# Thirty-two experts in an order found on the chip, the two largest run twice on one set of weights

## The chip, the cores and the metric

The kernel runs on one core of one Trainium2 chip. The metric is device time in microseconds (us) of one execution; lower is better. TensorE (PE in the profile) multiplies, PEld is its weight load, VectorE is DVE, ScalarE is ACT, GpSimd is POOL, and SyncE (SP) issues most DMAs.

## The reference, cut to what matters

The reference runs two transformer layers and a third block that ends in a mixture of experts. Only the mixture is touched. 512 tokens choose 4 of 32 experts each, so there are 2048 rows of work, and an expert with more than 128 tokens needs more than one block of 128 rows:

```python
logits = (xt @ router_w + router_b).astype(jnp.float32)
top_logits, top_idx = lax.top_k(logits, TOP_K)
gates = jax.nn.softmax(top_logits, axis=-1)
...
hmid = xt[tok] @ w_gu[e] + b_gu[e]             # 1024 -> 2048
glu = jnp.minimum(hmid[:, 0::2], SWIGLU_LIMIT)
lin = jnp.clip(hmid[:, 1::2], -SWIGLU_LIMIT, SWIGLU_LIMIT)
act = glu * jax.nn.sigmoid(SWIGLU_ALPHA * glu) * (lin + 1.0)
return act @ w_down[e] + b_down[e]             # 1024 -> 1024
```

All is float32. With the inputs of the reference the router gives expert 10 152 tokens and expert 12 130; eleven more experts have 65 to 124, and nineteen have 64 or fewer.

## The kernel before

The mixture is `experts`. `out_norm_and_route` finds the gates, each token's place in its expert (`T.place`) and the counts (`T.counts`, as integers `T.count`). `first_blocks` runs the first 128 tokens of experts 0 to 31 in their own order. `extra_blocks` runs what is left over, and `combine_and_finish` fetches four result rows for each token, adds them with the gates and normalises.

An expert's weights are six units of 2 MB (`expert_unit`): 0 to 3 are the two halves of the up projection, 4 and 5 the down projection. They go through a ring of eight slots (`ring_view`, `Home`); the first slot is named `unit_whole`. SP loads unit n of the next expert when the unit that held the slot, eight loads earlier, is used (`unit_used`, L4183).

An expert is one step, and each engine branches in it on the count (`is_half`, a register loaded from `T.count`, L4198). With 64 tokens or fewer the step is a **half** step: `up_half` and `down_half` multiply plain float32 in two column groups of 64 at once. Otherwise it is a **parted** step: unit 0 is multiplied in plain float32 (L3900), units 1 to 5 as three products of parts that ACT rounds (L88) and DVE subtracts (L91), quarter by quarter (L3870, L3871, L3875). Expert 0 alone has an unparted full path, `up` and `down`, in plain float32.

Rows of the next expert are fetched by an indirect DMA of POOL (L3575) and turned by PE (`turn_rows`, L3590), one half behind the up projection and one behind the turning of the activations (L3711 in a half step, L3883 in a parted one). `find_tokens` (L3559) makes the index three experts ahead.

The loop stands in `in_rounds`: experts 0 to 3 written out, a `Fori` over six rounds of four, experts 28 to 31 written out. While expert 0 is waited for, DVE works out which extra blocks there are (`Extras.find`, `find_jumps`). An extra block loads all six units of its expert again: for the first one SP issues them behind expert 31's, for a second one as the first's are used. The extra blocks' loop always makes 15 passes and skips those that are not needed.

Of the kernel before, what the change touches and what calls it, by code (L numbers as in the profile page):

```python
# [5 lines left out]
ALU = mybir.AluOpType  # L6
# [8 lines left out]
P = 128  # L15
# [1006 lines left out]
def mlp(k, i, gain, clear_rows=False):  # L1022
# [15 lines left out]
    with ExitStack() as ctx:  # L1038
# [19 lines left out]
        with k.block() as block:  # L1058
# [35 lines left out]
            def _(act):  # L1094
                if clear_rows:
                    act.wait_ge(k.pool_made.sem, k.pool_made.at(1))
                for n, (u, is_up, j) in enumerate(order):
                    k.round_unit(act, u + 1)
                    if clear_rows:
                        rows = k.rows[3 * n:min(3 * n + 3, BLOCKS)].rearrange("b p d -> p b d")  # L1100
                        act.dma_start(rows, zero[:, :, :].broadcast_to([P, rows.shape[1], D])).then_inc(k.rows_cleared, 16)
# [2362 lines left out]
BLOCKS = EXPERTS + MOST_EXTRA  # L3464
# [3 lines left out]
SLOTS = 8  # L3468

# [32 lines left out]
class Experts:  # L3502


    def __init__(self, k, name, tables, one_by_one):
# [6 lines left out]
        self.loaded = [signal(f"loaded{r}") for r in range(SLOTS)]  # L3512
        self.sel_ready = signal("sel_ready")
        self.index_full = signal("index_full")
        self.index_ready = signal("index_ready")
        self.fetched = [signal(f"rows_fetched{r}") for r in range(2)]
# [16 lines left out]
    def make_sel(self, dve, j, par):  # L3533
# [4 lines left out]
        for t in range(TT):  # L3538
            ins = dve.tensor_scalar(T.sel[:, par, t, :], T.iota[:, :], T.place[:, t, bass.ds(j, 1)], None, ALU.is_equal)
# [95 lines left out]
    def save_act(self, act, j):  # L3635
        k, T = self.k, self.tables
        act.wait_ge(self.act_turned, 2 * j + 2)
        act.activation(T.actT[:, :, :].rearrange("p (b f) s -> p b (f s)", b=2), k.psum[:, 4:6, :], ACT.Copy)\
           .then_inc(self.actT_ready, 2)
# [33 lines left out]
    def up(self, pe, j, home, xg, par):  # L3673

        k, T = self.k, self.tables
        for pair in range(2):
            for r in range(2):
                w = home.wait(pe, 2 * pair + r)
                for g in range(2):
# [4 lines left out]
                    for c in range(HALF_K):  # L3684
                        pe.matmul(bank, xg[:, HALF_K * r + c, :], w[:, c, g * 512:(g + 1) * 512],
                                  start=(r == 0 and c == 0), stop=False)
# [101 lines left out]
    def down(self, pe, j, home, par):  # L3788
        k, T = self.k, self.tables
        self.wait_for_down(pe, j)  # L3790
        for r in range(2):
            w = home.wait(pe, 4 + r)
            for half in range(2):
                bank = k.psum[:, 6 + half, :]
                cols = slice(half * 512, (half + 1) * 512)
                for c in range(HALF_K):
                    pe.matmul(bank, T.actT[:, HALF_K * r + c, :], w[:, c, cols], start=(r == 0 and c == 0), stop=False)
# [207 lines left out]
def experts(k):  # L4005

    with ExitStack() as ctx:
# [3 lines left out]
        T.place = k.sb("moe_place", [P, TT, BLOCKS], ctx=ctx)  # L4011
        T.iota = k.sb("moe_iota", [P, P], ctx=ctx)
# [5 lines left out]
        T.count = k.sb("moe_count", [P, EXPERTS], I32, ctx=ctx)  # L4018
# [7 lines left out]
        T.index = k.sb("moe_index", [P, EXPERTS], I32, ctx=ctx)  # L4026
# [9 lines left out]
        with ExitStack() as inner:  # L4036
# [21 lines left out]
            first_blocks(k, base, T, extras, later)  # L4058
# [4 lines left out]
class Extras:  # L4063
# [4 lines left out]
    def __init__(self, k, T, ctx):  # L4068
        self.k, self.T = k, T
        self.known = k.ctx.enter_context(k.nc.semaphore("extras_known"))  # L4070
        self.flag = k.sb("extra_flag", [P, ROUNDS - 1, EXPERTS], ctx=ctx)
# [18 lines left out]

    def find(self, dve):
# [5 lines left out]
        step(ins)  # L4097
        dve.memset(self.zero[:, :], 0.0)
# [18 lines left out]
    def fill(self, dve, t):  # L4117
# [5 lines left out]
        k.dve.step(dve, self.look_up(dve, self.cand[:, 0], T.place[:, t, EXPERTS:BLOCKS]))  # L4123

    def find_jumps(self, dve):
# [5 lines left out]
        step(dve.tensor_tensor(self.jump[:, 1, :], order[:, 0, :], T.ids[:, :], ALU.subtract))  # L4131
        step(dve.tensor_scalar(self.jump[:, 1, :], self.jump[:, 1, :], float(EXPERTS - 1), float(P), ALU.add, ALU.mult))
        step(dve.tensor_tensor(self.jump[:, 2:, :], order[:, 1:, :], order[:, :-1, :], ALU.subtract))
# [19 lines left out]
def first_blocks(k, E, T, extras, later):  # L4153
# [3 lines left out]
    PER_ROUND = 4  # L4157
    rounds = EXPERTS // PER_ROUND
    k.unit_rounded.passed(len(k.units))
    k.unit_split.passed(len(k.units))  # L4160
    with k.block() as block:
        def in_rounds(eng, step):

            for b in range(PER_ROUND):
                step(0, b, b, True, False)
            with eng.Fori(1, rounds - 1) as i:
                for b in range(PER_ROUND):
                    step(i, b, PER_ROUND * i + b, False, False)
            for b in range(PER_ROUND):
                step(rounds - 1, b, PER_ROUND * (rounds - 1) + b, False, True)  # L4170

        @block.sync
        def _(sp):
            def step(i, b, j, first, last):
                if last and b == PER_ROUND - 1:
                    return
# [565 lines left out]
```

## Time and profile before

| | us |
|---|---|
| median of 3 runs (lowest, highest) | 3099.53 (3092.92, 3102.09) |
| the profiled execution | 3098.87 |
| its span, first to last instruction | 3097.1 |
| experts 1 to 31, from store to store of the results | 1023.9 |
| the two extra blocks | 96.0 |

The page of the profile gives busy time of each engine (PE 89% of the span, DVE 52%, ACT 34%), the span in 40 slices, the chain of work that ended last, and the costliest groups of instructions. In a row of a timeline the first number is the start, the second the duration, and square brackets hold the engine's idle time before the row and who ended it. The issue of a result store on ACT is taken as the end of a step.

### The profile page before, as it was taken

How to read it: one execution, taken by the hardware profiler on the slowest of the kernel's cores; microseconds unless marked ns; L12 is line 12 of the kernel's file. 1: busy time of each engine (PE TensorE's matmuls, PEld its weight loads, DVE VectorE, ACT ScalarE, POOL GpSimd, SP SyncE). 2: the span in 40 equal slices, each digit the busy share in tenths (PEclk: the TensorE clock that was granted, in tenths of full speed). 3: DMA queues.
4: the chain of work that ended last, by engine and by line, in shares of the span. 5: the costliest groups of instructions: out<-in, count | busy, mean ns of one | idle time of the engine just before them, and what ended most of it. 6: DMA issues, size and time to landing. Idle time of an engine off the chain costs nothing. (4 is left out here: it accounts for less than half of the span.)

```text
span 3097.1 us, 35668 instructions
## 1 busy us (share of the span) xinstructions
PE 2741.5 (89%) x13162; PEld 1970.5 (64%) x13163; DVE 1614.4 (52%) x2447; ACT 1047.0 (34%) x1464; POOL 193.8 (6%) x213
## 2 busy tenths in 40 slices
PE   7877999999999899999966876998989998899962
PEld 6655778888878788888754663553655455455530
DVE  4864545444555544446855536652855454464413
ACT  4444443322224432233333231330634233343301
POOL 0530000000000000000012130000000000000002
PEclk9988999999999999999976787999999999999986
DMA  3110314444233132322210038999999999999974
GB/s 131 58 51 28 109 62 177 171 169 183 101 120 111 66 116 82 109 82 71 103 60 1 1 122 329 404 414 414 413 385 380 361 412 370 414 412 395 415 291 151
DMA packets 192096, 638.46 MB, mean 206 GB/s; under 512 B 12413, under 2 KB 18204, under 8 KB 191522
## 3 DMA queue, kind: packets, MB, share of 16 engines
q1 hardware_dynamic: 173856, 579.61, 48.7%
q10 hardware_dynamic: 11106, 39.11, 3.2%
q0 software_dynamic: 6912, 16.68, 1.4%
q8 instruction: 151, 2.47, 0.3%
q14 instruction: 71, 0.58, 0.1%
HBM read 600.61 MB, written 43.25 MB: 208 GB/s over the span
## 5 line engine op out<-in xcount | busy, mean ns | idle before, releaser
L91 DVE TENSOR_TENSOR unit_low<-unit_whole,unit_high 128x4096 fp32r<-128x4096 f32 (+3 forms) x95 | 287.8, 3035 | 174.8 <-ACT unit_high L88 172.9
L669 PE MATMUL psum<-tokens_high,unit_high 128*128 128x512 f32 (+2 forms) x1016 | 372.5, 367 | 4.4 <-PEq L865 1.6
L669 PE MATMUL psum<-tokens_high,unit_low 128*128 128x512 f32 (+2 forms) x1016 | 368.7, 363 | 0.0
L669 PE MATMUL psum<-tokens_low,unit_high 128*128 128x512 f32 (+2 forms) x1016 | 368.6, 363 | 0.0
L88 ACT ACTIVATE unit_high<-unit_whole 128x4096 fp32r<-128x4096 f32 (+2 forms) x65 | 225.8, 3474 | 374.2 <-PE psum L669 291.3
L91 DVE TENSOR_TENSOR moe_low<-ring_slot,moe_w_high 128x1024 fp32r<-128x1024 f32 x228 | 266.7, 1219 | 19.4 <-ACT moe_w_high L88 18.4
L88 ACT ACTIVATE moe_w_high<-ring_slot 128x1024 fp32r<-128x1024 f32 x228 | 236.5, 1055 | 61.4 <-PE psum L3875 60.4
L3698 PE MATMUL psum<-ring_slot,hT 128*64 128x512 f32 x1136 | 251.9, 594 | 0.0
L669 PEld LDWEIGHTS psum<-tokens_high,unit_high 128*128 128x128 f32 (+1 forms) x1016 | 191.0, 188 | 37.9 <-DVE unit_low L91 4.0
L669 PEld LDWEIGHTS psum<-tokens_low,unit_high 128*128 128x128 f32 (+1 forms) x1016 | 191.1, 188 | 31.6 <-issue 1.6
L669 PEld LDWEIGHTS psum<-tokens_high,unit_low 128*128 128x128 f32 (+1 forms) x1016 | 191.0, 188 | 30.6 <-issue 0.2
L669 PE MATMUL psum<-unit_high,hidden_high 128*128 128x512 f32 x512 | 199.7, 390 | 0.0
L669 PE MATMUL psum<-unit_high,hidden_low 128*128 128x512 f32 x512 | 199.4, 389 | 0.0
L669 PE MATMUL psum<-unit_low,hidden_high 128*128 128x512 f32 x512 | 199.4, 389 | 0.0
L3741 DVE TENSOR_SCALAR moe_glu<-psum 128x256 f32<-128x256 f32 x42 | 17.8, 425 | 324.4 <-PE psum L3704 232.7
L3698 PEld LDWEIGHTS psum<-ring_slot,hT 128*64 128x64 f32 x1136 | 83.5, 137 | 148.9 <-issue 147.7
L3726 PE MATMUL psum<-ring_slot,moe_actT 128*64 128x512 f32 x640 | 155.8, 641 | 9.7 <-ACT moe_actT L3766 9.7
L1147 DVE TENSOR_TENSOR x_residual<-psum,x_residual 128x512 f32<-128x512 f32 x128 | 84.4, 687 | 117.7 <-PE psum L669 117.7
L3870 PE MATMUL psum<-moe_w_high,moe_xg_high 128*128 128x512 f32 x312 | 131.1, 420 | 0.0
L3755 ACT ACTIVATE moe_sig<-moe_glu 128x256 f32<-128x256 f32 x42 | 17.5, 416 | 316.0 <-DVE moe_glu L3741 316.0
L3871 PE MATMUL psum<-moe_low,moe_xg_high 128*128 128x512 f32 x312 | 122.1, 391 | 0.0
L1137 DVE SCALAR_TENSOR_TENSOR hT<-psum,hidden_relu 128x512 f32<-128x512 f32 x64 | 43.8, 689 | 147.3 <-ACT hidden_relu L1109 147.3
(646 smaller groups left out, 4908.9 us busy)
## 6 DMA issues: line engine op xcount, KB each, us to landing
ring_slot<-in_moe_w_gu SPq DMA_DIRECT2D x118, 2048.0 KB, 19.4
ring_slot<-in_moe_w_down SPq DMA_DIRECT2D x60, 2048.0 KB, 20.5
unit_whole<-in_moe_w_gu SPq DMA_DIRECT2D x18, 2048.0 KB, 16.9
unit_whole<-in_w_up SPq DMA_DIRECT2D x16, 2048.0 KB, 7.5
unit_whole<-in_w_down SPq DMA_DIRECT2D x16, 2048.0 KB, 7.7
expert_rows<-zero_row ACTq DMA_DIRECT2D x15, 1536.0 KB, 5.3
unit_whole<-in_moe_w_down SPq DMA_DIRECT2D x8, 2048.0 KB, 19.7
unit_whole<-in_w_in SPq DMA_DIRECT2D x5, 2048.0 KB, 7.7
```

The source lines that it names most:

```text
L88: return act.activation(self.high, self.whole, ACT.Copy)
L91: return dve.tensor_tensor(self.low, self.whole, self.high.bitcast(F32), ALU.subtract)
L669: ins = pe.matmul(bank, a, c, start=(first and m == 0), stop=(last and m == len(parts) - 1))
L1137: dve.scalar_tensor_tensor(out=hidden[j % 2].whole[:, b, :], in0=bank, scalar=0.0, in1=relu[:, h % 2, :], op0=ALU.max, op1=ALU.mult)\
L1147: dve.tensor_tensor(x, bank, x, ALU.add).then_inc(k.bank_free.sem, 1)
L3698: ins = pe.matmul(banks[g], xg[:, c, 0:HALF], w[c // HALF_K][:, c % HALF_K, g * 512:(g + 1) * 512], start=(c == 0), stop=False)
L3726: ins = pe.matmul(banks[g], T.actT[:, c, 0:HALF], w[c // HALF_K][:, c % HALF_K, g * 512:(g + 1) * 512], start=(c == 0), stop=False)
L3741: dve.tensor_scalar(T.glu[:, pair, :], bank[:, :, 0], 7.0, None, ALU.min).then_inc(self.glu_ready, 2)
L3755: act.activation(T.sig[:, pair, :], T.glu[:, pair, :], ACT.Sigmoid, scale=1.702).then_inc(self.gate_ready, 2)
L3870: pe.matmul(banks[g], a.high[:, f, :], w.high[:, cols], start=(first and q == 0), stop=False)
L3871: pe.matmul(banks[g], a.high[:, f, :], w.low[:, cols], start=False, stop=False)
```

## The change

1. DVE sorts the experts by count on the chip (`put_in_order`): compare each with each (32x32), sum, and pick expert and count for each of 34 steps by a table of ranks. Results are the integer tables `T.order`, `T.column`, `T.count`, and a semaphore `ordered`.
2. There are 34 steps. Step 0 is expert 0 as before. Steps 2 and 3 are both the largest expert, steps 29 and 30 both the second largest; step 3 and step 30 run its tokens from the 129th on, with the weights that are still in the ring. From step 4 to 28 large and small experts take turns.
3. Steps 2, 3, 29 and 30 are of kind "whole": a full one is multiplied by `up` and `down` in plain float32 instead of in parts.
4. SP, ACT and DVE load the expert's number into a register in each step (`expert_at`, `column_at`).
5. PE turns both halves of the next rows behind the up projection.
6. Extra blocks are only those beyond the two second blocks; their prefetch in `first_blocks` is gone.

```diff
+AT_SECOND = (3, STEPS - 4)
+RANKS = [EXPERTS - 1, 26, 0, 0, 27] + [r for m in range(12) for r in (2 + m, 14 + m)] + [1, 1, 28, 29, 30]
...
+    for q, b, kind in ((0, 0, "first"), (1, 1, "parted"), (2, 2, "whole"), (3, 2, "whole"), (4, 3, "parted")):
+        step(Step(q, 0, b, kind))
+    with eng.Fori(1, ROUND_LAST) as i:
+        for b in range(PER_ROUND):
+            step(Step(PER_ROUND * i + b + 1, i, b, "parted"))
+    for q, b, kind in ((0, 0, "whole"), (1, 0, "whole"), (2, 1, "parted"), (3, 2, "parted"), (4, 3, "parted")):
+        step(Step(STEPS - 5 + q, ROUND_LAST, b, kind))
...
+        def expert_at(eng, q):
+            return eng.value_load(T.order[0:1, bass.ds(q, 1)], min_val=0, max_val=EXPERTS - 1)
...
+            sp.wait_ge(extras.ordered, 1)
+            load(Home(E, 0, 1), 1, (None, 0))
+            load(Home(E, 0, 2), 2, (0, 1))
+            load(Home(E, 0, 3), 4, (1, 3))
+            load(Home(E, 0, 4), 5, (3, 4))
...
-                    E.turn_rows(pe, j + 1, 0, 1 - par, (PER_ROUND // 2) * i + (b + 1) // 2 + 1)
+                if s.has(1):
+                    E.turn_rows(pe, q + 1, 0, 1 - par, s.fetches())
+                    E.turn_rows(pe, q + 1, 1, 1 - par, saved=q + 3 if s.has(2) else STEPS)
                 with pe.If(half):
-                    E.turn_act_half(pe, j)
+                    E.turn_act_half(pe, q)
+                    E.down_half(pe, q, home, par, counted)
...
+            E.make_sel(dve, 0, 0, 0)
             E.save_tokens(dve, 0)
+            E.make_bias(dve, 0, 0)
+            extras.put_in_order(dve)
+            E.make_sel(dve, 1, 1, column_at(dve, 1))
             E.save_tokens(dve, 1)
...
+                elif s.kind == "first":
+                    rows = 0
+                else:
+                    rows = expert_at(act, q)
```

What this moves, engine by engine. **PE, one step of the loop**, on its half path. Before, behind the up projection's bias (L3704), `hT` in L3590 being the next rows and L3711 the turning of the activations:

```order
L3590 MATMUL psum<-ident,hT 128x128 x4
L4226 COMPARE_AND_BRANCH
L3709 REGISTER_ALU
L3711 MATMUL psum<-ident,moe_act 128x128 x4
...
L3590 MATMUL psum<-ident,hT 128x128 x4
L4235 COMPARE_AND_BRANCH
```

After, in the same place, where L3626 turns the rows and L3752 the activations:

```order
L3626 MATMUL psum<-ident,hT 128x128 x4
L3622 REGISTER_ALU
L3626 MATMUL psum<-ident,hT 128x128 x4
L4326 COMPARE_AND_BRANCH
L3750 REGISTER_ALU
L3752 MATMUL psum<-ident,moe_act 128x128 x4
```

The second four turnings have moved ahead of the branch, and one branch of three is gone. **DVE, the start of the expert stage**, before; `moe_sel` is the one-hot table of an expert's tokens and `moe_index` its list:

```order
L3539 TENSOR_SCALAR moe_sel<-moe_iota,moe_place 128x128 x8
L3566 TENSOR_SCALAR moe_index<-psum 128x1 x2
L3539 TENSOR_SCALAR moe_sel<-moe_iota,moe_place 128x128 x4
L3597 COPY moe_bias_ones<-moe_bias_pick 128x128
L3605 TENSOR_TENSOR hT<-psum,feature_vectors 128x512 x2
```

And after:

```order
L3602 TENSOR_SCALAR moe_index<-psum 128x1
L3633 COPY moe_bias_ones<-moe_bias_pick 128x128
L4149 SCALAR_TENSOR_TENSOR extra_order<-moe_counts,moe_ids 128x32
L4151 MEMSET extra_order 128x1
L4152 TENSOR_TENSOR extra_prod<-extra_order 128x1024
L4154 TENSOR_REDUCE moe_rank<-extra_prod 128x32
L4156 TENSOR_TENSOR extra_prod<-moe_rank,moe_ranks 128x1088
L4158 TENSOR_TENSOR extra_prod<-extra_prod,moe_ids 128x1088
L4159 TENSOR_REDUCE moe_by_step<-extra_prod 128x34
```

The ordering stands between the first expert's index and the second expert's table, and the first expert's rows are saved (`hT`) behind both. **ACT, between two steps of the loop**, before and then after; L3650 and L3689 issue the store of the last results:

```order
L3650 DMA expert_rows<-moe_o 128x1024
L4315 UNCONDITIONAL_BRANCH
L4198 ISA
L4198 TENSOR_LOAD moe_count
L4198 ISA x2
L4311 COMPARE_AND_BRANCH
```

```order
L3689 DMA expert_rows<-moe_o 128x1024
L4415 UNCONDITIONAL_BRANCH
L4262 ISA
L4262 TENSOR_LOAD moe_order
L4262 ISA x2
L4259 REGISTER_ALU
L4259 TENSOR_LOAD moe_count
L4259 ISA x2
L4411 COMPARE_AND_BRANCH
```

A second register load stands ahead of the step's first activation.

## Rows read from the trace of the kernel before

**Rows 1.** Waits of PE, 1925.7 to 2949.6: us in total, times, longest

```profile
PE psum L3711 <- DVE moe_act L3748: 29.6, 18, 2.2
PE psum L3875 <- DVE moe_actT_low L3944: 11.8, 13, 1.0
PE psum L3870 <- ACT moe_actT_high L3979: 11.7, 13, 0.9
PE psum L3900 <- issue: 11.2, 3, 3.8
PE psum L3726 <- ACT moe_actT L3766: 9.0, 17, 0.8
PE psum L3698 <- issue: 5.6, 2, 3.8
```

**Rows 2.** Stretches: bounds, length, busy PE, PEld, DVE, ACT, POOL, then clock, DMA share, GB/s

```profile
1925.70:2949.60 1023.90, 943.68 (x4206) 530.89 (x4202) 539.57 (x863) 373.07 (x459) 31.57 (x29) 0.98 1.00 399
...
2047.90:2088.00 40.10, 38.25 (x166) 27.38 (x166) 32.40 (x39) 25.03 (x27) 1.23 (x1) 1.00 1.03 415
...
2113.90:2141.10 27.20, 23.79 (x114) 9.67 (x110) 5.66 (x17) 2.67 (x6) 0.99 (x1) 0.94 1.02 412
...
2556.80:2602.50 45.70, 41.32 (x168) 28.74 (x170) 32.63 (x39) 24.92 (x27) 1.23 (x1) 0.96 0.96 365
...
2857.10:2882.50 25.40, 23.46 (x114) 8.53 (x111) 4.78 (x13) 2.67 (x6) 0.99 (x1) 1.00 1.03 413
...
2949.60:3045.60 96.00, 64.30 (x340) 33.79 (x340) 11.40 (x30) 5.55 (x13) 0.00 (x0) 0.86 0.52 207
3045.60:3056.10 10.50, 0.00 (x0) 0.00 (x0) 0.00 (x0) 0.20 (x1) 0.00 (x0) 0.65 0.11 25
```

**Rows 3.** Stores of the experts' results, half steps and full ones, ns and starts

```profile
L3778 ACTq DMA_DIRECT2D expert_rows<-moe_o x21: 483/502/563, 1925.7 to 3045.6; - x21
...
L3650 ACTq DMA_DIRECT2D expert_rows<-moe_o x13: 343/359/374, 1994.9 to 2922.3; - x13
```

**Rows 4.** Timeline of PE in a half step

```profile
2094.01 0.60 PE L3698 MATMUL psum<-ring_slot,hT 128*64 128x512 f32 x2
...
2100.88 0.39 PE L3704 MATMUL psum<-moe_bias_parts,moe_bias_ones 128*64 128x512 bf16 x2
...
2103.42 0.66 PE L3711 MATMUL psum<-ident,moe_act 128*128 128x128 f32 x4 [1.57 <-DVE moe_act L3748]
2103.91 0.60 PE L3590 MATMUL psum<-ident,hT 128*128 128x128 f32 x4
2105.09 0.65 PE L3726 MATMUL psum<-unit_whole,moe_actT 128*64 128x512 f32 x2 [0.57 <-ACT moe_actT L3766]
```

**Rows 5.** Timelines of ACT, DVE and PE at the start of a parted step

```profile
2353.95 1.06 ACT L3844 ACTIVATE moe_xg_high<-hT 128x1024 fp32r<-128x1024 f32 x1 [1.83 <-issue]
...
2356.19 2.36 DVE L91 TENSOR_TENSOR moe_low<-ring_slot,moe_w_high 128x1024 fp32r<-128x1024 f32 x2
...
2357.46 0.75 PE L3870 MATMUL psum<-moe_w_high,moe_xg_high 128*128 128x512 f32 x1
```

**Rows 6.** Register loads of the count on ACT, ns and starts

```profile
L4198 ACTq TENSOR_LOAD <-moe_count x31: 273/283/365, 1932.7 to 2922.7; - x31
```

**Rows 7.** Timeline of DVE at the start of the expert stage

```profile
1878.36 0.21 DVE L3566 TENSOR_SCALAR moe_index<-psum 128x1 int32<-128x1 f32 x1
...
1894.74 1.66 DVE L4103 TENSOR_TENSOR extra_pick<-extra_order,moe_nth 128x1440 f32<-128x1440 f32 x1
...
1906.22 0.18 DVE L4115 CAST moe_ints<-extra_num 128x17 int32<-128x17 f32 x1
...
1908.54 0.43 DVE L3741 TENSOR_SCALAR moe_glu<-psum 128x256 f32<-128x256 f32 x1 [1.13 <-issue]
```

**Rows 8.** Timeline of PE: turning the first expert's rows

```profile
1890.19 1.97 PE L3590 MATMUL psum<-ident,hT 128*128 128x128 f32 x8 [11.23 <-DMA hT<-y_rows,moe_index]
```

**Rows 9.** Page, DMA issues: KB each, us from issue to landing

```profile
ring_slot<-in_moe_w_gu SPq DMA_DIRECT2D x118, 2048.0 KB, 19.4
```

## What the change will do to the time, predicted before it was run

> **What bounds the kernel now.** Only the expert stage changes, so I read it as a chain of steps and ask who waits. The slices of the page show the 16 DMA engines full there, and that invites the reading that weights set the pace. The waits of PE say otherwise: from expert 1's start to expert 31's store PE stands still 80 us in all, for DVE, for ACT and for "issue", and no wait is for a DMA [rows 1]. In a step of 40.1 us PE is busy 38.25 [rows 2]. So PE and its short waits on ACT and DVE are the pace, and the full DMA queue is prefetch that runs ahead until the ring is full.
>
> The steps have fixed prices. A half step takes 25.4 us, a parted one 40.1 [rows 2]. The stores count 21 half and 13 full steps, of which 19 and 13 are first blocks and two half ones are the extra blocks [rows 3]. 18 x 25.4 + 13 x 40.1 = 978.5. The stretch took 1023.9 [rows 2]; 16.8 of the rest are five waits for "issue" of up to 3.8 [rows 1], one at each jump back of the loop (expert 20's step, 45.7 instead of 40.1, is one [rows 2]). The rest, 28.6, is mostly TensorE's clock: its mean is 0.98 in the stretch, and single steps show 0.94 or 0.96, a short fall to 1.2 GHz that costs 27.2 - 25.4 = 1.8, and 45.7 - 40.1 - 3.8 = 1.8 in expert 20's step [rows 2]. By the ledger and the 0.98 that is about 13 such falls. Behind the loop the two extra blocks take 96.0 [rows 2], since their weights, gather and arithmetic come one after the other.
>
> **The change, part by part**, against the profiled execution's own time; it is 3098.87, the span 3097.1, the median 3099.53, so a difference carries over as it is.
>
> *The extra blocks go.* Both are half, so each belongs to an expert of its own with a full first block. These two have the highest counts, and steps 3 and 30 take both. -96.0.
>
> *Two half steps come.* Their weights lie in the ring, and a half step in the chain costs 25.4 whoever loads. +50.8.
>
> *Two full steps become whole.* No row shows an expert's full step in plain float32. In a half step eight pairs of such products take 2100.88 - 2094.01 = 6.87, 0.86 a pair, the two of a pair at once [rows 4]; 24 pairs are 20.6 of the 25.4, and 4.8 is turning, biases and waits. A whole step has 48 products one after another, 41.2, and 4.8, and four more turnings (0.49 [rows 4]) and larger copies on ACT (0.4): 46.9. Against 40.1 that is 6.8, twice, +13.6. Bounds 0 (as fast as parted) and 22 (four longer waits).
>
> *Both halves turned together.* In a half step the first four turnings lie in the wait for the activations, of which 1.57 is still left, and the second four lie in the wait for ACT's copy, 0.57 left [rows 4]. Moved, they shorten the first wait by 0.49 and lengthen the second by as much: nothing. In a parted step the second four lie ahead of down unit 5, whose first product already waits for ACT 0.9 behind them (13 times, 11.7 [rows 1]); that wait starts from the end of unit 4, and unit 4 now begins 0.49 later with nothing to hide it. 11 parted steps, +5.4. Bounds 0 and 6.
>
> *The expert's number in a register.* On DVE and SP the loads fall into time in which they wait for PE. On ACT one stands ahead of the first activation of each step. In a half step ACT has long to spare. In a parted one the chain ACT, DVE, PE is tight: DVE's first quarter ends 2356.19 + 1.2 = 2357.4, and PE takes it at 2357.46 [rows 5]. The load itself is 0.28 [rows 6], and register arithmetic goes with it; the whole idle time in front of the activation, with store issue, load and two branches, is 1.83 [rows 5]. I take 0.6, between 0.3 and 1.2. It shows in six parted steps, since five of the eleven stand at a jump back, where PE is 3.8 late itself. +3.6, bounds 0 and 13. By the Trainium skill (Runtime: NRT & Kernel Launch, Instruction fetch mechanics) such a register load is about 200 ns; the row has 283, and with 200 alone the term would be 1.2.
>
> *The start.* The sort stands on DVE behind the first index, saved at 1878.36 [rows 7]. It has eight wide operations of 1024 to 1088 elements: 1440 take 1.66 [rows 7], so about 1.2 each, 9.9; some eleven small ones at 0.2 (0.18 and the gap) [rows 7], 2.2; and two register loads that do wait, 0.9 each of the 1.13 that load and branch take together [rows 7], 1.8. So it ends near 1893, and behind it the second expert's table (load and four comparisons, 1.8), for which PE waits ahead of turning the first expert's rows: 1895.5. Before, that was at 1890.19, held by the fetch of the rows, for which PE stood 11.23 [rows 8]; so +5.3. DVE then has two more loads and six more small operations, 3.3, before it can activate, and it was the late one there. +8.6, bounds 3 and 13. The second expert's weights are issued some 15 us later, when DVE is done sorting; they are needed only at the second step, near 1934, and landing takes 19.4 [rows 9], so nothing comes of it.
>
> *The order.* If weights set the pace, turns of large and small would even out the demand. Since no wait is for them [rows 1], the order gives nothing. It does put a half step ahead of each jump back: 5 x 3.8 for 16.8, +2.2. *The held weights.* SP can load two units during steps 2 and 3 and gets the next slots 7 us into step 3; the next step needs unit 2 at 25.4 + 7 = 32 and has it at 7 + 19.4 = 26.4 [rows 2, 9]. Hidden, with 6 us to spare.
>
> *The clock.* It fell in about one in three steps, and in each long wait. With two more steps and longer waits in the parted ones I take 16 falls for 13, +5.4, bounds -5 and +15. *The end.* The 10.5 us behind the last store [rows 2] hold the store's landing and 13 skipped passes of the extra loop; now there are 15, and a load of their count: +1.6, bounds 0 and 3.
>
> Sum: -96.0 + 50.8 + 13.6 + 5.4 + 3.6 + 8.6 + 2.2 + 5.4 + 1.6 = -4.8. 3099.53 - 4.8 = 3094.7, say 3095. Two sets of weights fewer, and hardly a gain: what was loaded again is now multiplied longer.
>
> **The rivals.** *The covers hold.* ACT's load and the moved turnings cost nothing (-9.0), and the falls stay at 13 (-5.4): 3095 - 14.4, 3081. For it: each term is a fraction of a microsecond, and DVE or ACT may have slack that one timeline doesn't show. Against it: PE already waits at both places [rows 1, 5].
>
> *The clock falls in nearly every step*, and this one ends on the other side. The half step's pause of 1.57 and 0.57 [rows 4] becomes two of about 1.1 with a few products between, a parted step gets another pause at its start, and whole steps have two. If each of the 33 steps behind the first has a fall, that is 17 more than in my sum, 17 x 1.8 = 31: 3126. From eight more on the change is slower by more than 0.3%. Against it: the two pauses of a half step sum to what they were.
>
> *Weights do set the pace.* Then the added blocks hide behind the loads, and the loop doesn't lengthen: -96.0 + 8.6 + 1.6 = -85.8, 3014. Only the full DMA share speaks for it [rows 2]; the waits of PE speak against it.
>
> *Branches cost a fetch.* PE's half path now jumps over one long alternative, the whole down projection in parts, where it jumped over two shorter ones. If the 20 half steps behind the first each wait 3.8 as at a jump back [rows 1], +76: 3171. Against it: the jump over the up projection's alternative is longer still, and no such wait shows behind it: of the waits for issue there are five [rows 1], all at the loop's jump back. The Trainium skill (Runtime: NRT & Kernel Launch, Instruction fetch mechanics) has the rule that a taken branch whose target isn't in the current window of instructions waits for a fetch; by it a longer jump could cost, and the five waits at the jump back agree with it, the jumps inside a step do not reach it.
>
> *It doesn't do what it says*: another expert gets the second block, and an extra block of 48 (half of 96.0 [rows 2]) stays. 3095 + 48 = 3143. The counts leave no room for it.
>
> **How the numbers follow.** My forecast, 3084 to 3106 by the nearer bounds of its terms, 0.53. The covers hold 0.31. Clock 0.08. Weights 0.03. Branches 0.03. Another expert 0.02. A measurement of this kernel can tell about 0.3%, 9.3 us, from no change, so faster is below 3090.2 and slower above 3108.8. The covers and the weights are faster, 0.34; the clock, branches and another expert slower, 0.13; 0.53 is within. The range takes in the covers' 3081 with its start bound, and the clock's half way: 3076 to 3112.
>
> **What would show it.** Right: no row of an extra block; the sort's 1024 and 1088 wide rows on DVE end near 1891; first store near 1934; half steps of 25.4 to 25.9, parted ones of 40.6 to 41.3, steps 2 and 29 near 47; five waits for issue of 3.8; still none of PE for a DMA; last store near 3039. Wrong: whole steps above 52 or under 42, a wait of PE for a ring slot behind step 3, issue waits inside steps, a mean clock under 0.95 in the loop, or parted steps still at 40.1.

## The result, and the profile after

The changed kernel takes 3125.69 us (median of five runs, 3122.85 to 3128.75), the one before 3099.53 beside it: 1.0086 times as long, 95% interval 1.0071 to 1.0102. The forecast was 3095, from 3076 to 3112, so the change is slower by 26 us where no difference was expected, and 31 us above the forecast. The profiled executions differ by 24.0 us, 3121.1 against 3097.1.

Where the 24.0 us lie can be told by three points of both traces: the last product of TensorE that counts tokens (at 1873.8 before and 1877.3 after), the first store of an expert's results, and the last.

| stretch, us | before | after | forecast of the difference | measured |
|---|---|---|---|---|
| up to the last token count | 1873.8 | 1877.3 | 0 | +3.5 |
| to the first store | 51.9 | 58.2 | +8.6 | +6.3 |
| first to last store | 1119.9 | 1123.7 | -15.0 | +3.8 |
| last store to the end | 51.5 | 61.9 | +1.6 | +10.4 |
| sum | 3097.1 | 3121.1 | -4.8 | +24.0 |

The first line is taken as no effect of the change: nothing was touched there, and over all runs below that stretch varied between 1867.9 and 1886.5, which is also why differences of a few microseconds between single executions say little. Two lines missed, the chain of steps by 18.8 us and the end by 8.8.

The waits of TensorE in the chain of steps (us in total, times, longest), to be held against [rows 1]:

```profile
PE psum L3943 <- issue: 43.6, 5, 9.0
PE psum L3752 <- DVE moe_act L3789: 23.7, 20, 2.2
PE psum L3767 <- ACT moe_actT L3807: 18.8, 20, 1.0
PE psum L3913 <- ACT moe_actT_high L4022: 11.9, 9, 1.3
PE psum L3918 <- DVE moe_actT_low L3987: 5.9, 11, 0.7
PE psum L3913 <- DVE moe_low L91: 3.1, 4, 1.3
```

Still no wait is for a DMA, as forecast. But the five waits for issue, 16.8 us before, are 43.6: up to 9.0 each, all ahead of L3943, the first product of a parted step. Stretches from store to store, as in [rows 2] (bounds, length, busy PE, PEld, DVE, ACT, POOL, clock, DMA share, GB/s):

```profile
1935.50:3059.20 1123.70, 1008.02 (x4325) 530.57 (x4358) 500.35 (x868) 337.37 (x433) 33.30 (x31) 0.96 0.91 355
1962.80:2011.00 48.20, 45.84 (x122) 20.97 (x124) 11.86 (x41) 3.95 (x8) 0.99 (x1) 0.96 0.35 138
2107.90:2133.70 25.80, 23.66 (x118) 9.06 (x115) 5.65 (x17) 2.67 (x6) 0.99 (x1) 1.00 1.02 406
2201.60:2254.00 52.40, 42.54 (x165) 29.98 (x170) 32.62 (x39) 25.02 (x27) 1.23 (x1) 0.90 0.88 328
2279.80:2320.30 40.50, 38.50 (x163) 27.41 (x167) 32.40 (x39) 25.17 (x27) 1.23 (x1) 1.00 1.02 412
2906.00:2952.60 46.60, 44.25 (x122) 20.34 (x124) 8.69 (x25) 3.94 (x8) 0.99 (x1) 1.00 0.59 239
3059.20:3080.95 21.75, 0.00 (x0) 0.00 (x0) 0.00 (x0) 0.20 (x1) 0.00 (x1) 0.57 0.32 111
```

Most prices are those of the forecast: a half step 25.8, a whole one 46.6 (48.2 with a fall of the clock), a parted one 40.5. The fourth row is the exception. It is a parted step right behind the loop's jump back; there are five, of 52.3, 51.6, 51.5, 50.7 and 51.0 us, 51.4 in the mean. Against the ordinary parted step it has 7.9 us more in which TensorE stands still, and its products take 4.0 us more, since the granted clock is 0.90: a stretch of 6.8 us at 1.2 GHz begins at 2205.6, within the pause from 2200.3 to 2209.3, and another of 3.4 us lies 34 us behind it. In the other four such steps one stretch of 10.2 us is granted at 1.2 GHz.

The sequencer's own branches say what the standing still is. Two branches of TensorE in both kernels (durations min/median/max in ns): the loop's end, L4166 before and L3499 after, and the choice between the half and the full path in every step, L4218 before and L4314 after:

```profile
L4166 PEldq COMPARE_BRANCH  x6: 76/6056/6222, 2135.9 to 2827.2; - x6
L4218 PEldq COMPARE_BRANCH  x51: 65/240/1846, 1893.9 to 2931.0; - x51
```

```profile
L3499 PEldq COMPARE_BRANCH  x6: 67/6014/6273, 2196.4 to 2900.8; - x6
L4314 PEldq COMPARE_BRANCH  x55: 65/234/5392, 1901.3 to 3040.5; - x55
```

The jump back took 6.0 to 6.3 us in both, but for one of 3.6 before. New is that the choice between the half and the full path takes 4.8 to 5.4 us when it comes right behind it, five times; before, it took 0.24 there for the three full steps and 0.08 for the two half ones. TensorE's sequencer runs ahead of its products, so that of 6.3 and 5.4 us only 9.0 are left as a wait. ScalarE has a new stall as well. Its timeline across the first jump back, after (start, us, engine, line; in brackets the idle time):

```profile
2201.61 0.51 ACTq L3819 DMA_DIRECT2D expert_rows<-moe_o  x1
2211.03 1.06 ACT L3887 ACTIVATE moe_xg_high<-hT 128x1024 fp32r<-128x1024 f32 x1 [9.59 <-issue]
```

and across the second one before, which is also followed by a full step:

```profile
2280.01 0.51 ACTq L3778 DMA_DIRECT2D expert_rows<-moe_o  x1
2282.02 1.06 ACT L3844 ACTIVATE moe_xg_high<-hT 128x1024 fp32r<-128x1024 f32 x1 [2.18 <-issue]
```

From ScalarE's jump to its next instruction it is 6.1 to 6.8 us in each of the five rounds after, 0.24 to 0.26 before. VectorE has none: there it is under 0.1 us after.

At the end, the loop over extra blocks has nothing to run, but turns 15 times on each engine, and TensorE's first branch in it is a third long one:

```profile
L4437 PEldq COMPARE_BRANCH  x15: 214/221/6943, 3061.9 to 3079.4; - x15
```

The same branch before, which had run two blocks and then skipped 13:

```profile
L4335 PEldq COMPARE_BRANCH  x17: 75/214/222, 2969.6 to 3055.1; - x17
```

### The profile page after: what moved, and what is told of

Read it like the earlier page. It is cut to its first block and busy times, and to the rows that moved or that the text cites. A ratio compares the mean times of both kernels' runs of the same rounds, so it can differ in the third digit from the quotient of the medians.

```text
span 3121.1 us, 35734 instructions
## 1 busy us (share of the span) xinstructions
PE 2744.0 (88%) x12937; PEld 1939.0 (62%) x12979; DVE 1578.4 (51%) x2448; ACT 1005.7 (32%) x1425; POOL 196.9 (6%) x249
## 5 line engine op out<-in xcount | busy, mean ns | idle before, releaser
L3739 PE MATMUL psum<-ring_slot,hT 128*64 128x512 f32 x1184 | 262.1, 594 | 0.0
L91 DVE TENSOR_TENSOR moe_low<-ring_slot,moe_w_high 128x1024 fp32r<-128x1024 f32 x200 | 233.3, 1220 | 18.4 <-ACT moe_w_high L88 17.5
L88 ACT ACTIVATE moe_w_high<-ring_slot 128x1024 fp32r<-128x1024 f32 x200 | 208.0, 1056 | 59.2 <-PE psum L3918 58.5
L3767 PE MATMUL psum<-ring_slot,moe_actT 128*64 128x512 f32 x624 | 148.9, 632 | 16.9 <-ACT moe_actT L3807 16.9
L3767 PEld LDWEIGHTS psum<-ring_slot,moe_actT 128*64 128x64 f32 x624 | 51.0, 145 | 102.9 <-issue 96.5
L3913 PE MATMUL psum<-moe_w_high,moe_xg_high 128*128 128x512 f32 x264 | 109.5, 415 | 0.7 <-DVE moe_low L91 0.4
L660 PE MATMUL psum<-unit_high,high_parts 128*128 128x512 f32 (+2 forms) x256 | 99.3, 388 | 10.7 <-DVE low_parts L1997 4.4
## 6 DMA issues: line engine op xcount, KB each, us to landing
unit_whole<-in_moe_w_gu SPq DMA_DIRECT2D x16, 2048.0 KB, 10.1
```

Of the source, the lines that this page charges most:

```text
L88: return act.activation(self.high, self.whole, ACT.Copy)
L91: return dve.tensor_tensor(self.low, self.whole, self.high.bitcast(F32), ALU.subtract)
L660: ins = pe.matmul(bank, a, c, start=(i == 0 and m == 0), stop=(i == len(products) - 1 and m == len(parts) - 1))
L3739: ins = pe.matmul(banks[g], xg[:, c, 0:HALF], w[c // HALF_K][:, c % HALF_K, g * 512:(g + 1) * 512], start=(c == 0), stop=False)
L3767: ins = pe.matmul(banks[g], T.actT[:, c, 0:HALF], w[c // HALF_K][:, c % HALF_K, g * 512:(g + 1) * 512], start=(c == 0), stop=False)
L3913: pe.matmul(banks[g], a.high[:, f, :], w.high[:, cols], start=(first and q == 0), stop=False)
```

## The experiments

Theory A: the long waits are instruction fetches. A branch whose target isn't at hand costs some 5 to 6 us; after the change there are more such branches in a row, on TensorE and on ScalarE. Rival B: the steps behind the jump are slow through the moved rows, the register or the clock. Each run of the kernel before beside them gave 3097.2, 3097.5, 3100.7 and 3099.5 us; ratios are to these. "Less than the changed kernel" is against its 3125.7, measured beside 3099.5, so such a difference carries up to 2.3 us of shift.

That TensorE's long branches are fetches can be read from the DMA queues, which carry the instructions too. In each of the ten long branches of the changed kernel's loop one packet of 16 KB of queue 8 starts and ends, 1.4 to 1.6 us before the branch does; over the jump back (2196.4 to 2202.7) and the choice behind it (2203.5 to 2209.0):

```profile
q8 instruction: 1, 0.02, 1.0%
```

```profile
q8 instruction: 1, 0.02, 1.2%
```

Over the whole chain queue 8 carried 82 packets before and 83 after. So the second stall is hardly a block more to fetch, but a block that TensorE now has to wait for.

### The full path first, TensorE's loop written out, other places

**Full path first** (TensorE, first step of the loop's body):

```
-                with pe.If(half):
+                with pe.If(is_full(pe, s)):
                     E.wait_for_up(pe, q)
-                    E.up_half(pe, q, home, xg, par, counted)
+                    E.up_parted(pe, q, home, xg, par)
                 with pe.Else():
                     E.wait_for_up(pe, q)
-                    E.up_parted(pe, q, home, xg, par)
+                    E.up_half(pe, q, home, xg, par, counted)
```

> The changed kernel, with one edit on TensorE alone: in the first step of the loop's body the full path's up matmuls stand directly behind the branch and the half path's behind the Else, so that the long step that follows the jump back need not jump over the half path. Theory A (a second instruction fetch: the full path's target lies outside what was fetched for the jump back): the five branches of 4.8 to 5.4 us behind the jump back fall to about 0.2, the issue waits of L3943 from 9.0 to about 4 us each, and the steps behind the jump back from about 51.4 to 46 us; five such steps make 5 x 5.3 = 26 us, so about 3097 to 3101 us. Rival B (the long steps behind the jump are slow for another reason: the clock's falls, the expert's register, rows turned together): no change, 3123 to 3129 us.

3107.3 us, ratio 1.0032 (1.0021 to 1.0044): 18 us less than the changed kernel. The choice in the first step of the body (L4322), the choice in all others (L4328), and the step behind the first jump back:

```profile
L4322 PEldq COMPARE_BRANCH  x12: 68/236/422, 2057.8 to 2788.8; - x12
L4328 PEldq COMPARE_BRANCH  x49: 65/193/632, 1900.0 to 3019.8; - x49
```

```profile
2197.90:2244.90 47.00, 41.51 (x168) 28.67 (x170) 32.40 (x39) 25.03 (x27) 1.23 (x1) 0.96 0.96 365
```

No branch of 5 us is left on TensorE in the loop apart from the jump back, and the five steps take 47.3 us in the mean instead of 51.4, 20 us in all. That refutes rival B for this part; the rest, down to the 46 us expected, was not reached. The edit both puts the full path first and shifts the code behind it, so this run alone doesn't tell which of the two did it.

**TensorE's loop written out** (for that engine alone; in the kernel before likewise, in `in_rounds`):

```
-    with eng.Fori(1, ROUND_LAST) as i:
-        for b in range(PER_ROUND):
-            step(Step(PER_ROUND * i + b + 1, i, b, "parted"))
+    for i in range(1, ROUND_LAST):
+        for b in range(PER_ROUND):
+            step(Step(PER_ROUND * i + b + 1, i, b, "parted"))
```

> The changed kernel with TensorE's loop written out in full: no jump back on that engine, the same work in the same order, the other engines unchanged. Theory A: the five steps behind the jump back become ordinary parted ones of 40.5 to 42 us: 5 x (51.4 - 41) = 52 us less, about 3073 us, with no issue wait left in the loop and the granted clock at 1.00 there. If only the jump back itself is dear and a branch over the half path still costs a fetch each time (rival C), the 13 long steps keep some 5 us each and the time is 3105 to 3180 us. Rival B: the slow steps stay at 46 us or more, above 3095 us.

3106.3 us, ratio 1.0031 (1.0021 to 1.0041): theory A's time is missed by 33 us. The time lies in the ranges of rivals B and C, but C's mark isn't there: the longest branch in a step is 1.3 us, once, and the full steps other than the five take 40.7 to 42.1. The waits for issue are down to one of 1.2 us (L3948 here is L3943 of the changed kernel, L3918 its L3913), but the five steps stay at 49.1 us in the mean:

```profile
PE psum L3918 <- DVE moe_low L91: 31.8, 9, 6.3
PE psum L3757 <- DVE moe_act L3794: 23.7, 20, 2.2
...
PE psum L3948 <- issue: 1.2, 1, 1.2
```

Something else was waiting under them: TensorE runs through its first unit in plain float32 and then waits 5.4 us for the low parts of the next one, which VectorE makes from ScalarE's high parts; and ScalarE stands behind its own jump back, 5.8 to 6.1 us in each round.

> The kernel before with TensorE's loop written out in full, nothing else. Theory A: the five jump backs' 3.8 us go (16.8 us over the shortest steps, as three parted and two half ones) with the clock's falls behind them: 18 to 27 us less, 3073 to 3081 us. If the time of the jump back is covered by something else (a wait for ScalarE or a transfer that is late next), it stays at 3090 to 3100 us.

3092.6 us, ratio 0.9986 (0.9975 to 0.9998): 5 us instead of 18 to 27. The five steps behind the jump backs gave 15.5 us, and 8.4 were given back elsewhere. One place is the first extra block, 64.6 us for 58.5; another is expert 23, the third half step in a row (32.5 us for 25.7), where TensorE now waits for weights:

```profile
PE psum L3698 <- DMA ring_slot<-in_moe_w_gu: 4.9, 2, 2.9
PE psum L3711 <- DVE moe_act L3748: 1.5, 1, 1.5
PE psum L3726 <- DMA ring_slot<-in_moe_w_down: 0.5, 1, 0.5
```

**64 transposes that never run**, in the first expert's full path, ahead of the loop:

```
                         E.down(pe, q, home, par, counted)
+                    if s.kind == "first":
+                        for _ in range(64):
+                            pe.transpose(k.psum[:, 0, 0:P], T.y_of[:, 0, 0:P], k.ident[:, :])
```

> The changed kernel with 64 transposes added to TensorE's program in the one branch that is never taken (the first expert's full path), so that the loop's code lies 128 instructions further on and nothing else runs. If the second wait depends on where the loop's code lies against the fetched blocks (theory A), the five branches behind the jump back take another time than 4.8 to 5.4 us, or other branches take it, and the total moves by 5 us or more from 3125.7, to either side; if only the distance between branch and target counts (rival), it stays within 3 us of 3125.7.

3108.9 us, ratio 1.0039 (1.0025 to 1.0053), 17 us faster by adding instructions that nothing executes. The waits of L3943 for issue are 23.5 us for five instead of 43.6, and no branch of 5 us stands behind a jump back. In exchange the jump backs took 6.8 us for 6.0 to 6.3, one of 1.6 to 1.7 us appeared elsewhere in each of four rounds, and one of 4.5 us behind the loop's end. So the second stall depends on where the code lies.

### ScalarE, and all three engines

**The loop written out on TensorE, ScalarE and VectorE:**

> The changed kernel with the loop written out on TensorE, ScalarE and VectorE alike. With TensorE's alone written out the five steps stayed at 48.6 to 49.6 us, TensorE waiting 5.4 us for moe_low while ScalarE stood 6.1 us behind its own jump back. Theory A2 (after the change ScalarE's jump back costs a fetch too, which it did not before, and each engine's covers the other's): the five steps fall to 40.5 to 42 us, 5 x 7.5 = 38 us below the run with TensorE written out, about 3064 to 3072 us. Rival D (moe_low is late for its own work or for a transfer): the steps stay near 49 us and the time near 3106 us.

3064.0 us, ratio 0.9898 (0.9871 to 0.9924). The five steps take 41.1, 42.1, 40.7, 42.0 and 41.7 us; the waits of TensorE in the chain:

```profile
PE psum L3757 <- DVE moe_act L3794: 24.1, 20, 2.2
...
PE psum L3948 <- issue: 1.7, 2, 1.1
PE psum L3918 <- DVE moe_low L91: 1.2, 4, 0.5
```

```profile
1926.90:2999.20 1072.30, 1000.35 (x4325) 520.53 (x4358) 499.90 (x869) 337.94 (x433) 33.27 (x31) 0.98 0.94 372
```

The chain is 51.4 us shorter than the changed kernel's with the same work in the same order, the clock back at 0.98. With this the whole excess of the five steps is accounted for. VectorE had no stall at its jump back to lose, so what went is TensorE's and ScalarE's; the two alone were not run.

**ScalarE's loop alone written out:**

> The changed kernel with the loop written out on ScalarE alone. Theory A2: ScalarE's five waits of 6.1 to 6.8 us behind the jump back go, but TensorE's own 9.0 us (jump back and second branch) remain and are the longer ones: 3119 to 3126 us, little or nothing gained. If ScalarE's were the binding one (rival E), 3100 to 3112 us.

3123.5 us, ratio 1.0084 (1.0060 to 1.0108): nothing gained, the five steps take 51.2 us. Of two stalls side by side the longer one sets the time, and removing either alone (49.1 or 51.2) shows little of what removing both does (41.5).

**An unused register load, and 48 instructions that never run, on ScalarE before:**

```
+                if not (first or last):
+                    act.value_load(T.count[0:1, bass.ds(j, 1)], min_val=0, max_val=S)
```

> The kernel before, with one more load of a register on ScalarE in each of the loop's 24 steps, which nothing uses: its loop's body grows from 301 to 317 instructions, as long as it is after the change. Theory A2, by the body's length: ScalarE's jump back, 0.26 us before, takes 6 us, and the steps behind it grow by 1 us where TensorE's own 3.8 us cover it and by up to 5: 3100 to 3112 us. Rival F (the length does not matter, only the load's own 0.6 us): ScalarE's jump back stays at 0.3 us, and the time is 3097 to 3101 us.

3101.5 us, ratio 1.0019 (1.0004 to 1.0033). ScalarE's jump back stays at 0.24 to 0.27 us, so the length of the body, 317 instructions, isn't it; rival F holds. The median is 4 us above the kernel before. The chain took 1119.5 us in the trace, where it was 1119.9, but with 64.8 us at 1.2 GHz for 75.1; the loop's parted steps without a fall of the clock took 40.2 to 40.7 us for 40.1 to 40.2. So the load itself costs some 0.3 us a parted step.

```
                     E.save_down(act, j, j)
+                    if first and b == 0:
+                        for _ in range(48):
+                            act.activation(T.seen[:, :], k.ones[:, 0:1], ACT.Copy)
```

> The kernel before, with 48 instructions that never run in ScalarE's program ahead of its loop, nothing else. Theory P: the loop now lies where its 301 instructions reach over one more block, so ScalarE's jump back, 0.26 us before, takes 6 us in each of five rounds, and the steps behind the jump grow by 1 to 5 us: 3100 to 3112 us. Rival Q: 0.3 us as before, and 3095 to 3099 us.

ScalarE's jump back takes 6.07 to 6.21 us in all five rounds, where it took 0.25. The waits of ScalarE at the start of parted steps, in the kernel before and in this one:

```profile
ACT moe_xg_high L3844 <- issue: 23.3, 13, 2.2
```

```profile
ACT moe_xg_high L3844 <- issue: 43.3, 13, 8.3
```

The fetches themselves can be seen in the DMA queues. Packets of the instruction queues (with MB and share) from 2141 to 2152, the first jump back, before:

```profile
q8 instruction: 1, 0.02, 0.6%
```

and with the 48 instructions:

```profile
q8 instruction: 1, 0.02, 0.7%
q14 instruction: 3, 0.02, 0.6%
```

Over the whole chain queue 14 carried 41 such packets before and 67 here, 26 more in five rounds; the changed kernel has 72, 56 with ScalarE's loop alone written out and 38 with all three. The queue is therefore not ScalarE's alone. The time is still 3102.1 us, ratio 1.0002 (0.9988 to 1.0016): TensorE's own 3.8 us lie over most of it, and the three full steps behind a jump back went from 46.4, 45.7 and 45.7 to 46.2, 46.3 and 46.3. The fetch came as theory P said; its price, 1 to 5 us a step, did not, and the time lies in its range only because the kernel before beside it took 3100.7.

> The changed kernel with the full path first on TensorE behind the jump back (3107.3 us), and besides 128 instructions that never run in ScalarE's program ahead of its loop, so that its loop lies 128 instructions further on. Theory P (whether ScalarE's jump back costs a fetch depends on where the loop lies against blocks of the program: before, the body of 301 at its place was at hand, and so was one of 317 at the same place; the changed kernel's begins 19 instructions later and is not): at this place it is at hand again, ScalarE's 6.1 us go, the steps behind the jump fall from 47.0 to about 46 us or less, 3099 to 3104 us. Rival Q (what counts is the way the loop is written, not its place): the five waits of 6 us stay, 3105 to 3110 us.

3108.4 us, ratio 1.0025 (1.0011 to 1.0039): ScalarE's five stalls of 5.8 to 6.2 us remain. So place matters, as the 48 instructions show, but the rule by which I took 128 to be a good place is wrong, and no other was found.

### Rows turned together, the end, and the order

**The kernel before with both halves turned together** (the second `turn_rows` moved up behind the first):

> The kernel before, with both halves of the next expert's rows turned together ahead of the down matmuls, as the change has it, and nothing else of the change. The prediction's term: 14 parted steps x 0.49 us = 6.9 us more, 3100 to 3107 us, if the cover for ScalarE's high parts is gone. What the changed kernel's parted steps showed (40.5 us where 40.1 were): at most 14 x 0.2 us, 3095 to 3100 us.

3094.9 us, ratio 0.9994 (0.9985 to 1.0004); the chain is 1120.0 us for 1119.9. It costs nothing.

**The empty loop skipped:**

```
+            with eng.If(count > 0):
                 with eng.Fori(0, MOST_EXTRA) as b:
                     with eng.If(b < count):
```

> The changed kernel with one more branch: the loop over extra blocks, which now has none to run but still turns 15 times, is entered only if there is one. In the trace of the changed kernel TensorE spends 6.9 us on the loop's first branch and then 14 turns of 0.746 us, 10.4 us, after the last store, where the kernel before turned most of them under its last block. Theory G (these turns are on the path and are the 9 us by which the end grew): the branch of 6 to 7 us stays, the turns go, the end from last store to the span's end falls from 61.9 to about 51.5 us, and the time to 3113 to 3117 us. Rival H (the end is held by something else, a transfer or another engine's turns): 3122 to 3127 us.

3111.9 us, ratio 1.0038 (1.0025 to 1.0050), 14 us less than the changed kernel; from the last store to the end it is 49.8 us for 61.9. But the kernel before did not hide its turns under its last block: its 13 skipped passes ran from 3046.2 to 3055.5, behind the last store at 3045.6. Skipping them would be worth some 9 us there too; that was not run. The branch remains, now taken once:

```profile
L4436 PEldq COMPARE_BRANCH  x1: 5971/5971/5971, 3066.0 to 3066.0; - x1
```

> The changed kernel with the loop written out on TensorE, ScalarE and VectorE and the empty loop over extra blocks skipped: both remedies at once. If they add up: 3064.0 - 10.4 = 3053.6, 3050 to 3057 us, 1.4% below the kernel before.

3054.4 us, ratio 0.9854 (0.9829 to 0.9879): 71 us below the changed kernel and 46 below the one before, the best version found. Not all of the 46 is the change's: the kernel before was not run with both remedies. Its version without TensorE's jump backs, where ScalarE had no stall, has a ratio of 0.9986, the changed one with three loops written out 0.9898. By these two the change is worth some 27 us once the stalls are out of the way.

**Full experts first, then half ones:**

```
-RANKS = [EXPERTS - 1, 26, 0, 0, 27] + [r for m in range(12) for r in (2 + m, 14 + m)] + [1, 1, 28, 29, 30]
+RANKS = [EXPERTS - 1, 26, 0, 0, 27] + [r for r in range(2, 26)] + [1, 1, 28, 29, 30]
```

> The changed kernel with the loop written out on three engines (3064.0 us), and the 24 experts in the loop taken by falling count, eleven full ones and then thirteen half ones, not by turns. Theory R (the turns of full and half even out the demand for weights): a set of weights takes about 30.3 us at 415 GB/s, a half step 25.7, so of thirteen in a row all but the first two or three wait 4.6 us for a ring slot: 45 us more, 3105 to 3115 us, with TensorE waiting for DMA. Rival S, the prediction's (the order gives nothing): 3060 to 3068 us.

3123.5 us, ratio 1.0077 (1.0048 to 1.0107), 59 us more than with the turns of full and half. Now TensorE waits for weights:

```profile
PE psum L3744 <- DMA ring_slot<-in_moe_w_gu: 44.7, 18, 3.6
```

One of the last nine half steps of the loop, and the nine together, with what all DMA queues moved in the nine:

```profile
2651.60:2685.80 34.20, 25.48 (x118) 9.85 (x118) 5.56 (x17) 2.67 (x6) 0.99 (x1) 0.95 1.03 415
2619.90:2908.40 288.50, 228.14 (x1066) 87.24 (x1067) 50.40 (x153) 24.07 (x54) 8.90 (x9) 0.95 1.03 413
DMA packets 30915, 119.10 MB, mean 413 GB/s; under 512 B 1909, under 2 KB 1909, under 8 KB 30885
```

They take 32.1 us each instead of 25.7; the DMA moves 413 GB/s throughout. 9 x 6.4 is 58. My price was too low because it counted the weights alone, 12.6 MB a step: with the results and the gathered rows the queues moved 13.2 MB a step, which at 413 GB/s is 32.0 us. The clock, 0.95, has no part in it, since the queues were full throughout.

> The same order in the changed kernel as it is, with its loops. Two of the five jump backs now have a full step behind them and three a half one, which falls through to its path without the second branch: 3 x 5.3 = 16 us less than 3125.7, and by theory R the waits for weights, 4.6 us in each half step that has no jump back ahead of it, nine or ten of them less the first two: some 35 us more; together 3140 to 3150 us. Rival S: 3105 to 3112 us.

3154.5 us, ratio 1.0185 (1.0157 to 1.0213), a little above theory R's range, with 38.5 us of waits for the ring's slots. Against the falling order, taking full and half by turns is worth 29 us in the changed kernel and 59 with the loop written out. What the changed kernel would take in the order of the kernel before was not tried.

## Why the prediction was wrong

**The order, and the jump backs: wrong, the largest miss.** The term was "5 x 3.8 for 16.8, +2.2", with the step behind each jump back at its old price. It assumed that the wait of 3.8 us belongs to the jump. It belongs to the fetches that one pass over this place of the program has to wait for, and the change altered these. A full step now stands behind every jump back, and the branch to it waits for a fetch once more. Neither is enough alone: before, three of five jump backs had a full step behind them and no such wait; and in the changed kernel in falling order the choice took 2.4 and 4.7 us behind the two jump backs with a full step and 0.08 behind the three with a half one, though there, in two rounds, the jump over the full path in the same step took 3.2 us. With the code moved by 128 instructions it was 0.25 again. So it takes a full step behind the jump and the place of the changed code. The term was sized from the sum of the waits without asking what the wait consists of. Five steps of 51.4 us, where the sum had 40.1 + 0.5 + 3.8 + 1.8 = 46.2, are 26 us more than forecast.

**The rival on branches named the mechanism and put it in the wrong place.** It priced a fetch in all 20 half steps, +76, and was given 0.03. The sentence that failed is "the jumps inside a step do not reach it". Its support was that all five waits for issue stood at the jump back; but which branch a wait holds can't be read from the waits of TensorE. The rows of L4218 above could have been read in advance: 1.85 and 1.77 us in two steps of the kernel before, where the median is 0.24. The Trainium skill (Runtime: NRT & Kernel Launch, Instruction fetch mechanics) says that a taken branch to a target outside the current window stalls for a fetch, and that this is a reason for unrolling; the runs agree, with 4.8 to 6.9 us for each long branch of the changed kernel and 62 us for the loop written out on three engines. Why a target was at hand at one place of the code and not at another no run here shows.

**The register on ScalarE and the moved rows: too dear.** 5.4 for the rows in 11 parted steps and 3.6 for the register in six were forecast, 1.1 in each of these six; those without a fall of the clock took 40.5 for 40.1, 0.4 for both. Nearly all of it is the register's, whose load alone cost some 0.3 in the kernel before; the moved rows alone cost nothing there. So half of the rival that the covers hold was right. The cover for the moved rows, which I took to be gone, is there; what it consists of was not looked for. What the sum did not have is that the register's instructions also move ScalarE's loop in its program; the run with 48 instructions shows that such a move alone is enough for a fetch, though not that it was this in the changed kernel.

**The whole steps, half steps, extra blocks: right.** 46.6 for 46.9; 25.6 to 25.9; none of the 96.0 us is left.

**The start: right in mechanism.** The sort's wide rows end at 1892.5 (1891 forecast, in a trace that ran 3.5 us later there) and the stretch grew by 6.3 us for 8.6, within 3 to 13.

**The clock: right in number, wrong in length.** 16 stretches at 1.2 GHz were forecast and 16 are there, each of 3.4 us but for the five long steps, where one lasts 6.8 us and four 10.2: 85.3 us at 1.2 GHz in the chain, where the kernel before had 47.8 up to its extra blocks. The rival "the clock falls in nearly every step" gave 3126, the time that was measured, but by 33 falls; the agreement is chance.

**The end: wrong.** +1.6 became +10.4. The term counted two more turns and a load and left out that TensorE's first branch over the body, never executed now, isn't at hand: 6.9 us. The other 14 turns take 0.75 each, as the 13 before did, behind the last store as well. From the last store to the first of these branches, with the load of 0.9, it is 2.7 us; before it was 0.6, the load lying ahead of the extra blocks. So 6.7 for the branch, 1.5 for two turns and 2.1 for the load make up the 10.4.

**The held weights and "weights set the pace": right for this kernel only.** No wait for DMA in any version with turns of full and half. But "the order gives nothing" was drawn from there being no such wait before; what it showed is that the old order happened to be good enough under its stalls. With the loop written out the falling order loses 59 us, and the kernel before, once TensorE's stalls are gone, waits for weights in its runs of half steps (10.1 us in all).

In sum: the chain's miss of 18.8 us is 26 us in the five steps, less 4.1 for rows and register in the six other parted steps (0.4 for 1.1) and some 3 spread over the rest; the end's is 8.8; start and run-to-run differences are +1.2. Open stays where exactly a loop must lie for its jump back to find its target.

## What to carry to other kernels

Where a loop with paths chosen on the chip jumps back, list the durations of the sequencer's own branches on every engine, not only the waits of the busiest one: here each branch of 5 to 6 us held a fetch, they added up on one engine and hid one another across engines, so take them away on all engines at once before judging. Any edit that adds instructions or changes which path follows the jump can add one, far from the edit. And before trusting an order of large and small steps because nothing waits for a transfer, work out the rate that a run of small ones would need.

## What the runs showed of the hardware

- A fetch costs more than its wait: in the step with TensorE's wait of 9.0 us the granted clock was 0.90, with 10.2 us at 1.2 GHz, of which a part lay in the wait itself, and its products took 4.0 us more.
- Never-executed instructions changed which branches wait for a fetch: 128 to the better on TensorE (the choice behind the jump back from 4.8 to 5.4 us to 0.25, though the jump itself went from 6.0 to 6.8), 48 to the worse on ScalarE (0.25 to 6.1).
- The traffic of the instruction queues is in the profile: 16 KB a packet on queue 8, one within each of TensorE's ten long branches, and 8 KB on queue 14, whose count over the chain rose from 41 to 67 with ScalarE's five stalls alone. The number of packets doesn't tell the number of stalls: queue 8 had 82 without TensorE's second stall and 83 with it.
- An empty pass of a loop cost TensorE 0.75 us, and skipping a loop that had never run cost one branch of 6 us all the same.
